# Forgetting attention: the scores of three of the four head pairs, from one plain fp32 product per head on half the array to two whole-array passes of split operands

## The reference, cut to what matters

```python
def _fox_attention(q, k, v, log_f):
    c = jnp.cumsum(log_f, axis=1).transpose(0, 2, 1)
    scale = dh ** -0.5
    def block(i):                                   # 128 queries
        logits = jnp.einsum('bqhd,bkhd->bhqk', qb, k).astype(jnp.float32) * scale
        logits = logits + cq[..., :, None] - c[..., None, :]
        logits = jnp.where(mask, logits, NEG_INF)   # causal
        p = jax.nn.softmax(logits, axis=-1).astype(v.dtype)
        return jnp.einsum('bhqk,bkhd->bqhd', p, v)
```

## Time and profile before

| | us |
|---|---|
| median of 3 runs | 1925.45 (1924.77 to 1926.43) |
| the profiled execution | 1926.55 |
| its span, first to last instruction | 1924.8 |
| TensorE busy | 1903.9 (99%) |
| VectorE busy | 1177.6 (61%) |
| ScalarE busy | 835.9 (43%) |
| GpSimd busy | 27.1 (1%) |

### The profile page before, as it was taken

How to read it: one execution, slowest core, us unless ns; L and a number is a source line. 1 busy time by engine, 2 the same in 40 slices (tenths; PEclk the granted TensorE clock), 3 DMA queues, 4 the chain that set the end, 5 groups by cost and what they waited for, 6 DMA issues and landing times.

```text
span 1924.8 us, 30764 instructions
## 1 busy us (share of the span) xinstructions
PE 1903.9 (99%) x12192; PEld 1574.4 (82%) x12192; DVE 1177.6 (61%) x1927; ACT 835.9 (43%) x1359; POOL 27.1 (1%) x31
## 2 busy tenths in 40 slices
PE   9999999999999999999999999999999999999998
PEld 7776788888888888888888888877888778888887
DVE  6556577533655887757642564789988566425532
ACT  5447554333334565555332333465565543212232
POOL 0111000000000000000000000000000000000000
PEclk9999999999999999999999999999999999999999
DMA  6222123223223322222223222321211132322221
GB/s 223 77 69 77 63 72 108 76 99 109 89 89 129 93 78 80 88 107 71 105 82 115 88 85 90 114 75 57 72 47 50 63 110 87 110 88 91 105 88 66
DMA packets 33364, 172.42 MB, mean 90 GB/s; under 512 B 6968, under 2 KB 7128, under 8 KB 17376
## 3 DMA queue, kind: packets, MB, share of 16 engines
q1 hardware_dynamic: 28432, 165.49, 25.1%
q10 hardware_dynamic: 4816, 5.29, 0.9%
HBM read 163.39 MB, written 2.13 MB: 86 GB/s over the span
## 4 chain that ended last, share of the span: by engine, by line
PE 83%; DVE 9%; ACT 4%; issue 2%; DMA 1%; SPq 0%; DVEq 0%; ACTq 0%
PE bank L564 24%; PE bank L566 24%; PE bank L565 24%; PE bank L847 1%; ACT hH L1423 1%; PE bank L1215 1%; DVE hL L2255 1%; ACT wH L1423 1%; DVE x L2251 1%; PE bank L859 1%; PE bank L870 1%; PE bank L1059 1%; DVE wL L2176 1%; PE bank L1308 1%; DVE y L2764 1%
## 5 line engine op out<-in xcount | busy, mean ns | idle before, releaser
L564 PE MATMUL bank<-hH,wH 128*128 128x512 f32 x1368 | 549.2, 401 | 2.0 <-DVE hL L2217 1.6
L566 PE MATMUL bank<-hH,wL 128*128 128x512 f32 x1368 | 532.1, 389 | 0.0
L565 PE MATMUL bank<-hL,wH 128*128 128x512 f32 x1368 | 531.5, 389 | 0.0
L1423 ACT ACTIVATE wH<-raw 128x2048 fp32r<-128x2048 f32 (+4 forms) x199 | 293.5, 1482 | 117.6 <-PE bank L566 99.1
L564 PEld LDWEIGHTS bank<-hH,wH 128*128 128x128 f32 x1368 | 257.2, 188 | 55.9 <-issue 5.5
L2167 DVE TENSOR_TENSOR wL<-raw,wH 128x2048 fp32r<-128x2048 f32 x96 | 219.7, 2289 | 134.6 <-ACT wH L1423 134.6
L566 PEld LDWEIGHTS bank<-hH,wL 128*128 128x128 f32 x1368 | 256.9, 188 | 54.9
L565 PEld LDWEIGHTS bank<-hL,wH 128*128 128x128 f32 x1368 | 257.5, 188 | 47.8 <-issue 1.2
L564 PE MATMUL bank<-mH,wH 128*128 128x512 f32 (+1 forms) x610 | 232.8, 382 | 0.0
L565 PE MATMUL bank<-mL,wH 128*128 128x512 f32 (+1 forms) x610 | 232.6, 381 | 0.0
L566 PE MATMUL bank<-mH,wL 128*128 128x512 f32 (+1 forms) x610 | 232.6, 381 | 0.0
(11 more groups left out here) (386 smaller groups left out, 2828.5 us busy)
## 6 DMA issues: line engine op xcount, KB each, us to landing
raw<-in_ffn_up SPq DMA_DIRECT2D x44, 1024.0 KB, 4.8
raw<-in_mlp_up SPq DMA_DIRECT2D x16, 1024.0 KB, 4.8
raw<-in_mlp_down SPq DMA_DIRECT2D x16, 1024.0 KB, 4.8
raw<-in_ffn_down SPq DMA_DIRECT2D x16, 768.0 KB, 4.1
raw<-in_odd_in SPq DMA_DIRECT2D x12, 1024.0 KB, 4.8
raw<-in_dn_qkv SPq DMA_DIRECT2D x12, 1024.0 KB, 4.8
raw<-in_ffn_down SPq DMA_DIRECT2D x16, 640.0 KB, 3.9
raw<-in_even_in SPq DMA_DIRECT2D x7, 1024.0 KB, 5.0
```

What stands on the lines that cost most here:

```text
L564: mm(out, a, c, start=first, stop=False, skip_group_check=joined)
L565: mm(out, a, d, start=False, stop=False, skip_group_check=joined)
L566: return mm(out, b, c, start=False, stop=last, skip_group_check=joined)
L1423: return nc.scalar.activation(out, in_, func, **kw)
```

## The change

Pairs 0, 1 and 2 get their scores as in `diff_scores`; pair 3 keeps the plain product. New buffers: `fox_spare` (six tiles of 128 x 512: queries, high keys, low keys for each head of pairs 0 and 2) and, for pair 1, tiles that lie in the space of `qF`, `kF` and `vM` not in use then. ScalarE copies the high parts (`fox_high`), VectorE subtracts the low parts (`fox_low`; the queries' low part goes to the other half of the partitions), SyncE copies the keys to the other half (`fox_keys_both_ways`), and TensorE waits for both before a pair's first scores.

```diff
--- before.py
+++ after.py
@@ -206,6 +206,13 @@
         cq_at, qF_at = base + 4 * 5 * SEQ, base + 4 * (13 * SEQ + 2 * 1280)
         cqRaw = sb("cqRaw", [P, 5, SEQ], F32, cq_at)
         foxH, foxL = sb("foxH", [P, 4, SEQ], F32R, qF_at), sb("foxL", [P, 4, SEQ], F32R, qF_at + 4 * 4 * SEQ)
+        def single(name, tile):
+            return sb(name, [P, SEQ], F32R, qF_at + 4 * tile * SEQ)
+
+        spare, = [sb("fox_spare", [P, 6, SEQ], F32R)]
+        fox_q = ([spare[:, e, :] for e in range(2)], [single(f"fox_q{e}", 3 + 4 * e)[:] for e in range(2)])
+        fox_kH = ([spare[:, 2 + e, :] for e in range(2)], [single(f"fox_kH{e}", 18 + e)[:] for e in range(2)])
+        fox_kL = ([spare[:, 4 + e, :] for e in range(2)], [single(f"fox_kL{e}", 17 - e)[:] for e in range(2)])
         gate_rows = sb("gate_rows", [P, SEQ], F32, qF_at + 4 * 16 * SEQ)
         rank_inverse = sb("rank_inverse", [P, 2, SEQ], F32, qF_at + 4 * 18 * SEQ)
         qM, kM = sb("qM", [P, H, SEQ], F32, h_at), sb("kM", [P, H, SEQ], F32, h_at + 4 * H * SEQ)
@@ -286,6 +293,11 @@
         def pair_ends(t, delay):
             return [g for g in range(8) if pair_slot(4 * g + 3) + delay == t]
 
+        def fox_split_at(t, delay):
+
+            slots = ((36, 38), (43, 52), (75, 84))
+            return [(g, tl) for g in range(3) for tl in range(2) if slots[g][tl] + delay + (tl if g else 0) * (delay > 0) == t]
+
         def gate_slot(g):
             return (40, 40, 88, 106)[g]
 
@@ -500,6 +512,14 @@
                         sp.wait_ge(*at(f"diff.k_{kind}{h}.{e}"))
                         sp.dma_start(buf[part(1 - e), h % 2, e, :].bitcast(F32), buf[part(e), h % 2, e, :].bitcast(F32))\
                             .then_inc(*tick(f"keys_spread{h % 2}", f"diff.keys{h}" if (kind, e) == ("low", 1) else None, 16))
+
+            def fox_keys_both_ways(g):
+
+                for buf, kind in ((fox_kH, "high"), (fox_kL, "low")):
+                    for e in range(2):
+                        sp.wait_ge(*at(f"fox.k_{kind}{g}.{e}"))
+                        sp.dma_start(buf[g % 2][e][part(1 - e), :].bitcast(F32), buf[g % 2][e][part(e), :].bitcast(F32))\
+                            .then_inc(*tick(f"fox_spread{g}", f"fox.keys{g}" if (kind, e) == ("low", 1) else None, 16))
 
             sp.dma_start(vec[:, 0:8], dram["vec"][:, 0:8]).then_inc(*tick("loaded_gain", "in.gain", 16))
             first_weights(0)
@@ -520,6 +540,8 @@
                 if name.startswith("even_") and name != "even_out":
                     for j in range(2 if n0 == 0 else 0, units):
                         n = n0 + j
+                        if n in (5, 7, 9):
+                            fox_keys_both_ways((n - 5) // 2)
                         if n >= 2:
                             sp.wait_ge(w_split, n - 1)
                         load(name, n, j, n % 2)
@@ -828,8 +850,11 @@
                 else:
                     pe.wait_ge(evac, 4)
                 if i == TT - 1:
-                    if g < 4:
-                        pe.wait_ge(evac, 2 * (1, 2, 4, 8)[g] + 2)
+                    if g < 3:
+                        pe.wait_ge(*at(f"fox.queries{g}"))
+                        pe.wait_ge(*at(f"fox.keys{g}"))
+                    elif g == 3:
+                        pe.wait_ge(evac, 18)
                     else:
                         pe.wait_ge(*at(f"uq.nope{g - 4}"))
                         for e in range(2):
@@ -837,6 +862,12 @@
                             pe.wait_ge(*at(f"rope.placed{2 * (g - 4) + e}"))
                         pe.wait_ge(*at("rope.zero"))
                 for e in range(2):
+                    if g < 3:
+                        q = fox_q[g % 2][e][:, i * P:n]
+                        mm(bank[2 + e][:, 0:n], q, fox_kH[g % 2][e][:, 0:n], start=True, stop=False)
+                        mm(bank[2 + e][:, 0:n], q, fox_kL[g % 2][e][:, 0:n], start=False, stop=True)\
+                            .then_inc(*tick("pair_pe", f"pair.scores{m}.{e}"))
+                        continue
                     if g < 4:
                         q, k = qF[half(e), g, i * P:n], kF[half(e), g, 0:n]
                     else:
@@ -1705,6 +1736,16 @@
                 act.wait_ge(mm_done, 2 * n - 2 if n <= 10 else TILE0["even_uq"] + 3 * (n - 11))
                 hi_half(n, f)
 
+            def fox_high(g, tl):
+
+                evacuated("even_in", 2 * (1, 2, 4)[g] + tl)
+                if g == 2:
+                    act.wait_ge(*at("pair.scores3.1"))
+                for e in range(2):
+                    dst, src = (fox_kH, kF) if tl else (fox_q, qF)
+                    a(dst[g % 2][e][part(e), :], src[part(e), g, :], ACT.Copy)\
+                        .then_inc(*tick("fox_act", f"fox.{'k' if tl else 'q'}_high{g}.{e}"))
+
             def pair_exp(m):
 
                 for e in range(2):
@@ -1741,6 +1782,8 @@
                     for f in range(2):
                         if even_split_half(n, f) == t:
                             even_hi(n, f)
+                for g, tl in fox_split_at(t, 0):
+                    fox_high(g, tl)
                 if t == 219:
                     act.wait_ge(*at("pair.scores31.1"))
                     hi_half(14, 0)
@@ -2437,6 +2480,20 @@
                     ins = tt(misc[:] if l == 0 else cqRaw[:, {1: 0, 10: 1, 11: 2, 12: 3, 13: 4}[l], :], b[:], rinv, ALU.mult)
                 ins.then_inc(evac, 1)
 
+            def fox_low(g, tl):
+
+                for e in range(2):
+                    dve.wait_ge(*at(f"fox.{'k' if tl else 'q'}_high{g}.{e}"))
+                    if tl:
+                        if g == 1:
+                            dve.wait_ge(*at("gate.stored"))
+                        tt(fox_kL[g % 2][e][part(e), :], kF[part(e), g, :], fox_kH[g % 2][e][part(e), :].bitcast(F32), ALU.subtract)\
+                            .then_inc(*tick("fox_dve", f"fox.k_low{g}.{e}"))
+                    else:
+                        q = fox_q[g % 2][e]
+                        tt(q[part(1 - e), :], qF[part(e), g, :], q[part(e), :].bitcast(F32), ALU.subtract)\
+                            .then_inc(*tick("fox_dve", f"fox.queries{g}" if e else None))
+
             def pair_biased(m):
 
                 g, i = m // 4, TT - 1 - m % 4
@@ -2515,6 +2572,8 @@
                 for g in pair_ends(t, 11):
                     if g < 4:
                         pair_low(g)
+                for g, tl in fox_split_at(t, 2):
+                    fox_low(g, tl)
                 if t == 57:
                     dve.wait_ge(*at("in.rope"))
                     tt(sq[64:96, 1, :], misc[96:128, :], rope[96:128, 1, :], ALU.mult).then_inc(*tick("rope_dve", "rope.key_sin"))
```

## The result

| | kernel before | changed kernel |
|---|---|---|
| median of 20 runs each, us | 1925.70 (1924.77 to 1927.21) | 1928.52 (1927.62 to 1929.56) |
| ratio, 95% interval | 1 | 1.0014 (1.0008 to 1.0020) |
| profiled execution: its time, its span, us | 1926.55, 1924.8 | 1929.14, 1927.4 |
| mean granted clock of TensorE | 0.999 | 0.998 |

The change makes the kernel 2.8 us slower, 0.14%. That is less than the 0.2% which the prediction took as the bound of "no change that can be told", but with 20 runs a side the interval leaves out 1. The prediction's own time, 1925.8, was 2.7 us too low, and 1928.52 lies just above its range (1922.4 to 1928.4). Both were counted from a time before of 1925.45, and the kernel before itself came out at 1925.70 in the twenty runs. As a difference the forecast was +0.3, the range reached to +2.95, and the measured +2.8 lies just inside it.

The account below looks back on a forecast made before the run. TensorE, busy 32.00 of 32.00 us at full clock while pairs 0 and 1 run, was taken as the bound. Array saving -2.7 plus pair 0's wait +3.0 gave +0.3 on 1925.45, so 1925.8 us; range 1922.4 to 1928.4.

Parts of the forecast that it names:

- the saving in the array: TensorE's score tiles of pairs 0 to 2 get shorter: 0.86 us a pair, 2.7 in all, 2.3 at least.
- the 0.09 of the old form: Late start of old score tiles behind the projection matmul, 0.09 us, charged to all four tiles of a pair.
- The saving of the 128-key tile: Narrowest score tile goes from 0.52 to 0.39 us, saving 0.13; if nothing, the whole saving is 2.3.
- the old form's slow way out (0.10): Projection matmul after the first old tile takes 0.22 us to its successor instead of 0.12; charged to that tile only.
- where the wait is, and the chain up to it: Ahead of pair 0's first scores: last key subtraction ends at 44.05, TensorE starts at 46.5, having waited 3.0 us (2.7 to 3.5).
- the keys come in time: Rival at pair 0's first scores: no wait, the gain stands, 1922.75 us; chance 0.17 with the partial cases.
- VectorE's subtractions land on the path: Rival in all three pairs: TensorE waits for VectorE's work, up to 8.2 us on top of -2.7, 1931 us; chance 0.07.
- the landing of the last key copy: Pair 0's last key copy is issued at once and lands 2.2 us later, at 46.25; slowest landing 2.7.
- The rival of the late landing: Pair 0's key copies land late as `cB` or a weight load moves too; wait 6.2, time 1929.0 us; chance 0.08.
- The row of the copies up to 5.4: Profile row of SBUF to SBUF copies elsewhere, up to 5.4 us, by which TensorE would start at 49.7.
- the clock falls in the wait: Rival at pair 0's wait: TensorE's clock drops to 1.2 GHz, costing 2.2 us as a bound, 1928.0 us; chance 0.08.
- the gain in the array is paid back by one wait: Conclusion for the whole kernel: saving -2.7 plus pair 0's wait +3.0 gives +0.3 us; likeliest case, 0.60.

Follow-up runs that it names:

- the run with pair 0 left as it was: Changed kernel, but pair 0's scores go back to the two array halves, without its split and copies; 1924.25 us, ratio 0.9992.
- the later slots: Changed kernel with pair 0's scores at steps 55, 61, 67 and 73 instead of 48, 55, 62 and 69; 1922.82 us, ratio 0.9986.
- the load held back: Changed kernel with weight unit 5's 1 MB load on SyncE's queue waiting until pair 0's key copies have landed; 1928.59 us, ratio 1.0014.
- kept busy: Changed kernel with 17 products into a bank nobody reads, run by TensorE ahead of its wait for pair 0's keys; 1926.48 us, ratio 1.0007.
- with both: Changed kernel with unit 5's load waiting for pair 0's key copies and 12 unread products ahead of TensorE's wait; 1926.18 us, ratio 1.0002.
- the same move in the kernel before: Kernel before, old score format, with pair 0's four slots moved to steps 55, 61, 67 and 73; 1926.32 us, ratio 1.0003.

## Why the prediction was right and wrong

**Right, but half a us too small: the saving in the array.** In the changed kernel's timeline the tiles of 384, 256 and 128 keys of pair 0, and the one of 512 keys of pair 2, read:

```profile
54.47 0.28 PE L588 MATMUL bank<-wH,hL 128*128 128x256 f32 x1
54.59 0.34 PE L867 MATMUL bank<-fox_spare 128*128 128x384 f32 x1
...
55.29 0.93 PE L890 MATMUL bank<-const,prob 128*128 128x128 f32 x7
...
61.20 0.28 PE L867 MATMUL bank<-fox_spare 128*128 128x256 f32 x1
...
61.68 0.49 PE L890 MATMUL bank<-const,prob 128*128 128x128 f32 x3
...
67.20 0.22 PE L867 MATMUL bank<-fox_spare 128*128 128x128 f32 x1
...
67.60 0.62 PE L890 MATMUL bank<-const,prob 128*128 128x128 f32 x4
...
99.23 0.39 PE L867 MATMUL bank<-fox_spare 128*128 128x512 f32 x1
...
100.14 0.38 PE L890 MATMUL bank<-const,prob 128*128 128x128 f32 x2
100.27 0.48 PE L586 MATMUL bank<-hH,wH 128*128 128x512 f32 x1
```

From start to start: 0.70, 0.48, 0.40 and 0.91, where 0.71, 0.47, 0.39 and 0.90 were predicted; and the first score follows the projection by 0.12, so the 0.09 of the old form is gone. The saving of the 128-key tile, the least sure, is there too (0.40 for 0.52).

What the prediction missed is behind the tile. It charged the old form's slow way out (0.10) to the first tile only, "since the others are followed by transposes, which stay". They stay, but they were slower too. The same 512-key tile of pair 2 before:

```profile
96.34 1.13 PE L847 MATMUL bank<-kF,qF 64*128 64x512 f32 x4
97.40 0.44 PE L859 MATMUL bank<-const,prob 128*128 128x128 f32 x2
97.59 0.48 PE L564 MATMUL bank<-hH,wH 128*128 128x512 f32 x1
```

The two transposes take 0.19 there and 0.13 with the change (100.14 to 100.27). From the tile's start to the next projection product it is 1.25 and 1.04; with the 0.09 ahead the tile saves 0.30, where the prediction has 0.25. Over three pairs the saving is 3.2 instead of 2.7, as the trace of the run with pair 0 left as it was bears out (2.1 for two pairs, below). In time, the runs with the later slots in the new and in the old format stand at 0.9986 and 1.0003 of the kernel before, a difference of about 3.2 us, with some 1.7 us of uncertainty on either side of each.

**Right: where the wait is, and the chain up to it.** The last key subtraction of pair 0 ends at 43.37, in before's time 44.08, against 44.05 predicted. The wait is put down to the key copies, and there is none at the scores of pairs 1 and 2; VectorE's 20.65 us in the stretch against 17.34 cost nothing, as costed. The rivals "the keys come in time" and "VectorE's subtractions land on the path" fall.

**Wrong: the landing of the last key copy.** The prediction's step was "lands 2.2 later", from copies of another stage, and against more it argued that "the weight load stands behind the copies on the same queue". To stand behind them on the queue did not keep the load away: it was issued 0.50 us after the copy, and the copy took 3.53, so the term was mis-sized by 1.3, and the wait was 4.28 instead of 3.0. The rival of the late landing, at 0.08, came true in part. With the load held back the copy took 2.45 and 2.47, but with the load behind it also 3.2 and 2.3: the load can't be called the cause of the 1.1 us between 2.45 and 3.53 by these runs, and that cause stays open. The place on the queue was in any case no argument against a late landing. The row of the copies up to 5.4 bounded it. The copies of pairs 1 and 2, issued some 0.4 us behind a load of 1 MB, landed after 5.6 to 5.9 in the changed kernel; their scores stand so much later that TensorE did not wait for them, as the prediction had it.

**Wrong: the clock.** The rival "the clock falls in the wait" had 0.08, since no row of before showed it. It happened in both runs in which TensorE stood idle there (4.28 and 3.2 us), and in neither of those in which it was kept busy. The Trainium skill ("TensorE: Matmul & The Clock Gate", Part 1) was cited for the rule that idleness takes the clock back to 1.2 GHz; the trace agrees, with 0.50 granted from 47 to 50. The prediction had the mechanism and the rule that spoke for it, and named a falling clock among the signs that it is wrong. Its price of 2.2 was meant as a bound; the traces below give 1.5 in the changed kernel, and some 2.7 with the load held back. It gave the rival too small a chance: a wait of 3 us which it forecast itself was unlike anything in the trace of before, so that trace could not speak against it.

**The sum with the measured terms.** The terms can be followed in the traces. The last projection product ahead of the place of pair 0's first scores starts at 43.26 before, and the first one behind pair 2's last scores and transposes at 121.02, so 77.76 later:

```profile
121.02 0.36 PE L564 MATMUL bank<-wH,hH 128*128 128x256 f32 x1
```

In the changed kernel (from 42.55) and in the run with pair 0 left as it was (from 43.04) the same product starts here:

```profile
122.93 0.36 PE L586 MATMUL bank<-wH,hH 128*128 128x256 f32 x1
...
118.66 0.36 PE L586 MATMUL bank<-wH,hH 128*128 128x256 f32 x1
```

That is 80.38 and 75.62, so 2.62 later and 2.14 earlier than before: pairs 1 and 2 save 1.07 each, and three pairs 3.2. The two products start at 43.13 and 121.71 in the run kept busy, at 43.17 and 123.64 with the load held back, at 43.01 and 120.83 with both, at 43.15 and 117.82 with the later slots, at 43.21 and 121.23 with the same move in the kernel before. The clock's term is 0.46 of the time for which TensorE worked at 0.50, since a product took 0.43 there instead of 0.23.

| run | saving | wait | clock | sum | by the trace, behind pair 2 | by the time, against before beside it |
|---|---|---|---|---|---|---|
| changed kernel | -3.2 | 4.28 | 1.5 | +2.6 | +2.62 | +2.8 |
| kept busy | -3.2 | 3.98 | 0 | +0.8 | +0.82 | +0.8 |
| load held back | -3.2 | 3.2 | 2.8 | +2.8 | +2.71 | +2.95 |
| both | -3.2 | 3.22 | 0 | 0.0 | +0.06 | +0.3 |
| slots later | -3.2 | 0 | 0 | -3.2 | -3.09 | -2.8 |
| pairs 1 and 2 alone | -2.1 | 0 | 0 | -2.1 | -2.14 | -1.4 |
| same move before | 0 | 0 | 0 | 0.0 | +0.26 | +0.4 |

In the traces the sum holds within about 0.1 in every run but the last, where the move costs 0.26. The times lie up to 0.7 from the traces. A ratio is known here to some 0.09%, 1.7 us, and behind pair 2 the traces drift against each other (kept busy: +0.82 there and 0.0 at the end of the program; changed kernel: +2.62 and +3.3), so what half a us becomes by the end is not resolved.

From the forecast of +0.3 it is three steps to +2.6: the saving was 0.5 larger, the wait 1.3 longer, and the clock, which had no term in the sum, cost 1.5. The measured time lies inside the range, at its edge, only because the range took in the clock, a rival with a chance of 0.08; that the undersized saving took 0.5 off the other two errors is luck.

The step that failed last is the conclusion, "the gain in the array is paid back by one wait": the wait, with what it set off, cost nearly twice the gain (5.8 against 3.2).

## What to carry to other kernels

When a change makes TensorE wait where it never did, price the wait and the clock together: here 4.3 us of standing still were followed by 3.3 us at half speed. When a new operand needs a split and a copy, look first at the steps between its eviction and its use, and move the use if it has room: two numbers turned a loss of 2.8 us into a gain of 2.8. The landing of a small copy on the path is a term with a spread: the same copy landed after 2.3 to 3.53 in five traces, so price its longest row as well as its median.

## What the runs showed of the hardware that was not expected

- A copy of one tile's half from SBUF to SBUF landed in 2.45 and 2.47 us with the next load on its queue held back, and in 3.53, 3.2 and 2.3 with a load of 1 MB issued 0.5 us behind it. Issued some 0.4 us behind such a load, copies of the same size landed in 5.4 to 6.0 in every run that has them.
- Leaving the two half-array products cost TensorE time ahead of both things that followed them here: 0.10 ahead of a projection product, and 0.06 over the two transposes shown (0.19 instead of 0.13).
- The clock fell in a wait of 3.2 us as well as in one of 4.28, and the shorter wait was followed by the longer stretch at 0.50 (6.0 against 3.3 us of work). A shorter wait is therefore not always a gain: the two runs took 1928.59 and 1928.52. What sets the length of the slow stretch was not tried.
